# Four stages of a four-layer kernel reordered: gates first, keys and values turned early, attention waits by unit, and another order at the last attention's end

## The chip, the core and the metric

The kernel runs on one core of one Trainium2 chip. A core has five instruction streams that run side by side and meet only at semaphores: TensorE (matrix products, PE in the rows), VectorE (DVE), ScalarE (ACT), GpSimd (POOL) and SyncE (SP), which only issues transfers here. The metric is the device time of one execution in microseconds. Before the change three runs gave 2090.48, 2090.92 and 2097.49 us; the median is 2090.92 us.

## What is computed

Two blocks, one behind the other, of two layers each, on 256 tokens x and 256 context tokens, model width 1024, all in float32. Layers 0 and 1 (the first block) mix the tokens with a two-directional mLSTM, a gated spatial unit and a convolution; layer 2 mixes with windowed and dense attention, layer 3 with differential attention. Behind each mixer comes a SwiGLU feed-forward part. What the change touches, cut from the reference:

```python
def mlstm_inputs(p):
    q, k, v = heads(p[..., Q_OFF:K_OFF]), heads(p[..., K_OFF:V_OFF]) * HEAD_DIM ** -0.5, heads(p[..., V_OFF:O_OFF])
    g = p[..., GATE_OFF:SGU_OFF]                      # gates = (g0, log_sigmoid(g1), g2, log_sigmoid(g3))
def step(carry, inp):                                 # one chunk of 128 tokens of the mLSTM
    b = jnp.cumsum(fc, axis=-1)
    C_new = decay * C + einsum('bhsk,bhsv->bhkv', ks, vc)
    s = einsum('bhtk,bhsk->bhts', qc, kc) * exp(Dlog - m_t)
def one_block(args):                                  # layer 2
    p = _softmax(concatenate([s_c, s_w], axis=-1), sink_b)
    return einsum('bhgqk,bkhd->bqhgd', p[..., :n_ctx], v_ctx) + einsum('bhgqk,bkhd->bqhgd', p[..., n_ctx:], vw)
def _diff_attend(q, k, v, lam):                       # layer 3
    a = p[:, :, 0] - lam * p[:, :, 1]
    return einsum('bhqk,bkhe->bqhe', a, v)
def finish(o):
    return (_rms(o, subln_w) * (1.0 - lam_init)).reshape(o.shape[0], o.shape[1], -1) @ w_out
```

## The kernel before

The activations lie transposed in on-chip memory: 8 tiles of 128 rows (features) by 512 columns (256 tokens x, then 256 tokens of context). Layers 1 and 3 give out only the 256 tokens of x. Every large product is made of three products of rounded parts: weights and inputs are each split into a high part (ScalarE, `high_weights`) and a low part (VectorE, `low_weights`: the weight less its high part). The weights come in items of two tiles; ScalarE and VectorE split the item that comes next while TensorE multiplies the one before. In `coming_weights(L, e)` ScalarE's turn is at odd tiles e, VectorE's at even ones, and each half of an item has a semaphore count of its own.

There is no scheduler. Each engine's program is a Python function (`tensor_program`, `vector_program`, `scalar_program`, `pool_program`, `sync_program`), and its instructions run in the order in which they are written; an engine that waits holds back all that is behind it. The places that matter here:

- **mlstm_projection(L), layers 0 and 1.** 24 tiles e = 0 to 23. Behind tile 7 TensorE multiplies the gates' weights. ScalarE's `gate_activations` (five activations behind a table load) feed VectorE's `log_forget`, the scans `cumulated`, the running `maxima`, and then ScalarE's `row_exponents`, whose rows TensorE turns behind tile 15 (`gate_columns`). Tiles 12 to 19 (keys and values) are 512 wide in both layers. VectorE also applies the convolution's taps here (`conv_steps`). At the end stands a layer norm: means (`layer_norm_sums` part 0), centred (VectorE), squared (ScalarE), sums of squares (part 1), root, scaling, and silu (ScalarE).
- **mlstm(L).** First the keys and values of four heads are turned from features to tokens: TensorE turns into banks 0 to 3, VectorE copies the keys out, ScalarE the values; two heads fit into the banks at a time. Then the recurrent stage: TensorE spreads rows (64 x n), makes scores (128 x 128), outer and inner products, each in turn with VectorE's exponents and weighting, ScalarE's exponentials and GpSimd's scaled keys; modulation steps for later layers stand in between.
- **even_projection and even_mixer, layer 2.** Ten of the twelve projected tiles are normalised by head and rotated (three VectorE steps each, semaphore `rotated`). 24 units of attention follow, three to a tile (`kind` 0 to 2). For each: scores (TensorE), maximum (VectorE), exponential (ScalarE), reciprocal (VectorE), scaling of one half of the map by GpSimd and of the other by ScalarE (`even_weights`), turn, copy out, product. Units 0 to 2 are scored within the projection; the unit AHEAD = 3 further on is scored before unit n is turned.
- **odd_mixer, layer 3.** Behind the projection stand the last two maps (14 and 15), the products of heads 6 and 7, the squares, their bounding (`sub_bounded`) and their means (`sub_mean`) for heads 4 to 7, root and reciprocal (`sub_norm`), the spread of the factors over the rows (`sub_spread`), the normalised heads, their high (`odd_cut`) and low parts (`odd_low`), and the first half of the depth of the first four output tiles (`upper_mixed`).
- `keep_busy(b, n)` is n products of 128 x 128 into a bank that nobody reads.

In the names of the rows, `bank` is the accumulation memory, `big` and `scratch` are shared storage, `yT` and `rstd` hold squares, rows or statistics according to the stage, and `modulation_slots` holds attention's results in layer 3.

## Time and profile before

| | us |
|---|---|
| median of three runs | 2090.92 |
| lowest, highest | 2090.48, 2097.49 |
| profiled execution | 2094.34 |
| its span, from first to last instruction | 2092.9 |
| TensorE busy | 1999.8 (96%) |
| VectorE busy | 1394.4 (67%) |
| ScalarE busy | 1043.3 (50%) |
| GpSimd busy | 422.8 (20%) |
| mean granted TensorE clock | 0.993 |

Times in the rows are microseconds from the start of the span. A timeline row has start, duration, engine, line, operation, result <- inputs, shape, count, and in brackets the engine's idle time before it and the instruction that ended it. The lines of matrix products and turns are those of helpers (L780, L789), and so is L1526, a VectorE multiply-add. A float32 product of TensorE leaves two records, a turn one.

### The profile page before, as it was taken

What the parts mean: (1) busy time and instruction counts of PE and PEld (TensorE: products, weight loads), DVE (VectorE), ACT (ScalarE), POOL (GpSimd) and SP (SyncE); (2) the same over time, 40 slices, a digit from 0 to 9 for tenths busy, and PEclk for the clock granted to TensorE, in tenths of its full rate; (3) what the DMA queues carried; (4) which work ended last, traced back from release to release, by engine and by line L of the source; (5) the groups of instructions that cost most, each with busy time, mean ns of one, the idle gap of its engine ahead of it and who ended that gap; (6) DMA issues with size and microseconds to landing.
All of it is one profiled execution on the core that took longest, in us unless ns stands there. A gap on an engine that the chain in (4) does not pass through costs nothing.

```text
span 2092.9 us, 32728 instructions
## 1 busy us (share of the span) xinstructions
PE 1999.8 (96%) x12878; PEld 1683.1 (80%) x12878; DVE 1394.4 (67%) x2355; ACT 1043.3 (50%) x1948; POOL 422.8 (20%) x324
## 2 busy tenths in 40 slices
PE   6999999999999899999999999999999999999999
PEld 4776677888997777799986567798898877769999
DVE  4394647967987765655564674796798866666555
ACT  3445544542553555654455793454255256555443
POOL 1000415521541003200010241651254100000000
PEclk9999899999999999999999999999999999999999
DMA  9632521547458823556463102254832632114563
GB/s 337 227 141 81 172 70 50 193 136 258 147 172 258 302 84 108 196 185 197 144 199 121 61 2 89 81 187 117 273 101 89 227 110 73 61 61 157 166 208 115
DMA packets 276745, 311.65 MB, mean 149 GB/s; under 512 B 6128, under 2 KB 260208, under 8 KB 269424
## 3 DMA queue, kind: packets, MB, share of 16 engines
q1 hardware_dynamic: 271888, 304.90, 44.5%
q10 hardware_dynamic: 4704, 4.65, 0.7%
q8 instruction: 103, 1.69, 0.3%
q14 instruction: 50, 0.41, 0.1%
HBM read 308.48 MB, written 1.05 MB: 148 GB/s over the span
## 4 chain that ended last, share of the span: by engine, by line
PE 72%; DVE 13%; ACT 7%; POOL 3%; issue 3%; DMA 1%; ACTq 0%; DVEq 0%; POOLq 0%
PE bank L780 70%; DVE weights_low L1534 3%; PE bank L789 2%; ACT weights_high L2323 2%; DVE scratch L1526 1%; DVE weights_low L1915 1%; DVE yT L1526 1%; DVE input_low L1526 1%; DMA parameter_columns<-p_columns 1%; DVE big L2159 1%; ACT big L2856 1%; DVE big L1526 1%; DVE hidden_low L1929 1%; POOL token_sums_raw L673 0%; DVE token_sums L1920 0%
## 5 line engine op out<-in xcount | busy, mean ns | idle before, releaser
L780 PE MATMUL bank<-input_high,weights_high 128*128 128x256 f32 (+1 forms) x2336 | 749.4, 322 | 26.0 <-DVE scratch L1953 9.6
L780 PE MATMUL bank<-input_high,weights_low 128*128 128x256 f32 (+1 forms) x2336 | 736.0, 316 | 0.0
L780 PE MATMUL bank<-input_low,weights_high 128*128 128x256 f32 (+1 forms) x2336 | 714.5, 317 | 4.8 <-DVE input_low L1526 4.8
L1534 DVE TENSOR_TENSOR weights_low<-weight_slots,weights_high 128x1024 fp32r<-128x1024 f32 (+2 forms) x344 | 386.9, 1163 | 188.3 <-ACT weights_high L2323 188.0
L780 PEld LDWEIGHTS bank<-input_high,weights_high 128*128 128x128 f32 x2336 | 439.9, 188 | 83.4 <-issue 26.1
L780 PEld LDWEIGHTS bank<-input_low,weights_high 128*128 128x128 f32 x2336 | 434.0, 188 | 42.7 <-DVE input_low L1526 9.2
L780 PEld LDWEIGHTS bank<-input_high,weights_low 128*128 128x128 f32 x2336 | 440.0, 188 | 33.4
L2323 ACT ACTIVATE weights_high<-weight_slots 128x1024 fp32r<-128x1024 f32 (+2 forms) x348 | 314.5, 951 | 150.1 <-PE bank L780 137.0
L1915 DVE TENSOR_TENSOR weights_low<-weight_slots,weights_high 128x512 fp32r<-128x512 f32 x216 | 232.8, 1097 | 23.4 <-ACT weights_high L2601 21.5
L780 PE MATMUL bank<-hidden_high,weights_high 128*128 128x256 f32 (+1 forms) x704 | 238.5, 339 | 0.6 <-DVE weights_low L1534 0.4
L780 PE MATMUL bank<-hidden_high,weights_low 128*128 128x256 f32 (+1 forms) x704 | 237.4, 337 | 0.0
L780 PE MATMUL bank<-hidden_low,weights_high 128*128 128x256 f32 (+1 forms) x704 | 237.2, 337 | 0.0
L751 POOL TENSOR_TENSOR yT<-yT 128x256 f32<-128x256 f32 (+1 forms) x66 | 66.5, 1012 | 634.1 <-ACT yT L2349 504.4
L1526 DVE SCALAR_TENSOR_TENSOR xT<-bank,modulation,xT 128x256 f32<-128x256 f32 x144 | 64.4, 479 | 125.5 <-PE bank L780 124.7
L2601 ACT ACTIVATE weights_high<-weight_slots 128x512 fp32r<-128x512 f32 x216 | 129.3, 623 | 37.0 <-POOL weight_slots L696 19.0
L780 PEld LDWEIGHTS bank<-hidden_high,weights_high 128*128 128x128 f32 x704 | 132.1, 188 | 18.5 <-issue 1.9
L780 PEld LDWEIGHTS bank<-hidden_high,weights_low 128*128 128x128 f32 x704 | 132.1, 188 | 16.1
L780 PEld LDWEIGHTS bank<-hidden_low,weights_high 128*128 128x128 f32 x704 | 132.2, 188 | 15.8
L780 PE MATMUL bank<-token_sums,weights_high 128*128 128x256 f32 x576 | 105.2, 281 | 3.6 <-ACT scratch L2648 2.5
L691 POOL TENSOR_TENSOR weight_sum<-weight_slots 128x512 f32<-128x512 f32 x36 | 49.8, 1382 | 277.8 <-DVE weights_low L1915 135.6
L2349 ACT ACTIVATE yT<-xT 128x256 f32<-128x256 f32 (+1 forms) x64 | 32.9, 522 | 139.7 <-DVE xT L1526 134.2
L780 PEld LDWEIGHTS bank<-token_sums,weights_high 128*128 128x128 f32 x576 | 88.0, 188 | 5.0 <-ACT scratch L2648 3.4
(278 smaller groups left out, 2760.3 us busy)
## 6 DMA issues: line engine op xcount, KB each, us to landing
weight_slots<-w_gu SPq DMA_DIRECT2D x44, 1024.0 KB, 5.2
weight_slots<-ffn_w_in SPq DMA_DIRECT2D x44, 1024.0 KB, 5.2
modulation_slots<-p_modulation_rows SPq DMA_DIRECT2D x64, 512.0 KB, 4.7
modulation_slots<-mod_w SPq DMA_DIRECT2D x32, 1024.0 KB, 6.2
modulation_slots<-w_mod SPq DMA_DIRECT2D x28, 1024.0 KB, 6.3
weight_slots<-w_in SPq DMA_DIRECT2D x24, 1024.0 KB, 7.9
weight_slots<-w_down SPq DMA_DIRECT2D x16, 768.0 KB, 5.9
weight_slots<-ffn_w_out SPq DMA_DIRECT2D x16, 768.0 KB, 5.7
```

The source lines that it names most:

```text
L691: pool.tensor_tensor(m.weight_sum[:, :, :], a21, a22, ALU.add).then_inc(m.weights_added.sem, 1)
L751: pool.tensor_tensor(o, yT[:, 2 + q, t] if k == 1 else o, yT[:, 2 + i % 4, t], ALU.add).then_inc(m.square_joined.sem, 1)
L780: return pe.matmul(o, w, r, start=start, stop=stop, skip_group_check=shared)
L789: return pe.transpose(o, a, ident[0:a.shape[0], 0:a.shape[0]])
L1526: return stt(out=o, in0=a, scalar=s, in1=b, op0=op0, op1=op1)
L1534: tt(m.w_low[:, g % 2, c], m.ring[:, g % SLOTS, c], m.w_high[:, g % 2, c].bitcast(F32), ALU.subtract).then_inc(m.low_made.sem, 1)
L1915: tt(low, m.raw(run, j), high.bitcast(F32), ALU.subtract).then_inc(m.low_made.sem, 1)
L1929: tt(m.a_low[:, local, :], m.prod[:, f % 2, :], m.a_high[:, local, :].bitcast(F32), ALU.subtract).then_inc(m.hid_low.sem, 1)
L2159: dve.tensor_reduce(m.od_max[:, x % 2, a:a + 1], bank[2 + a][:, :], AX.X, ALU.max).then_inc(m.odd_max.sem, 1)
L2323: F(m.w_high[:, g % 2, c], m.ring[:, g % SLOTS, c], ACT.Copy).then_inc(m.high_made.sem, 1)
L2349: F(yT[:, 2 + k % 4, t], xT[:, k, t], ACT.Square).then_inc(m.squared.sem, 1)
L2601: F(m.split(j)[0], m.raw(run, j), ACT.Copy).then_inc(m.high_made.sem, 1)
```

## The change

1. Layer 1's gates: `gate_activations` stands ahead of tile 8's evacuation on ScalarE, and VectorE's low weights of the item that follows tile 10 stand ahead of the first scans.
2. Layers 0 and 1: the turns of heads 0 and 1 move between the last layer norm's two sums, with VectorE copying both their keys and values there; the values of heads 0 to 2 are copied by VectorE (semaphore `v_moved`), only those of head 3 by ScalarE. Behind the turns stand 14 `keep_busy` products.
3. Layer 2: the wait for all rotations is replaced by one per query tile; the first turn waits for the banks it needs. ScalarE's scaling of maps 0 and 1 moves ahead of unit 2's exponentials, with VectorE's second reciprocal ahead of it.
4. Layer 3: squares and bounds of heads 5 and 6 come earlier, cuts and low parts of heads 0 to 3 later, and the halves of the output tiles are spread between the means; the low weights of the second item stand inside the norm.

```diff
@@ TensorE, mlstm_projection and mlstm
-        for part in range(2):
-            layer_norm_sums(L, 1, part, n)
+        layer_norm_sums(L, 1, 0, n)
+        for h in range(2):
+            turn_keys_values(L, h)
+        layer_norm_sums(L, 1, 1, n)
+
+    def turn_keys_values(L, h):
+        for s, (tile, out_) in enumerate(((K_T, m.k_out), (V_T, m.v_moved))):
+            b = 2 * (h % 2) + s
+            if h > 1:
+                pe.wait_ge(*out_.at(L, h - 2))
+            else:
+                pe.wait_ge(*m.projected.at(L, 20 + b))
...
-        for h in range(HEADS):
...
+        for h in range(2, HEADS):
+            turn_keys_values(L, h)
+        keep_busy(5, 14)
         pe.wait_ge(*m.k_out.end(L))
+        pe.wait_ge(*m.v_moved.end(L))
         pe.wait_ge(*m.v_out.end(L))
@@ TensorE, layer 2
+        if n >= AHEAD and kind == 0:
+            pe.wait_ge(*m.rotated.at(2, 3 * (2 + n // 3) + 2))
...
+            elif half == 0:
+                pe.wait_ge(*m.head_root.end(2))
+            else:
+                pe.wait_ge(*m.rotated.at(2, 3 * (len(EVEN_NORMED) - 1)))
...
-        pe.wait_ge(*m.rotated.end(L))
@@ TensorE, layer 3
-        for h in (6, 7):
-            sub_mean(h)
-        upper_mixed(L, 0)
+        sub_mean(6)
+        upper_mixed(L, 0, (0,))
+        sub_mean(7)
+        upper_mixed(L, 0, (1,))
+        upper_mixed(L, 1, (0,))
         pe.wait_ge(*m.odd_keyed.end(0))
         for u in (2, 3):
             sub_spread(u)
-        upper_mixed(L, 1)
+        upper_mixed(L, 1, (1,))
@@ VectorE, layer 1 and both first layers
-            coming_weights(L, e)
+            if L == 0 or e != 10:
+                coming_weights(L, e)
...
+                    if s == 1 and L == 1:
+                        coming_weights(L, 10)
                     cumulated(L, (2 * s - 2, 2 * s - 1))
...
+        layer_norm(L, 1, 0, n)
+        for h in range(2):
+            keys_by_token(L, h)
+            values_by_token(L, h)
+        layer_norm(L, 1, 1, n)
@@ VectorE, layer 2 and layer 3
+            if e == 12:
+                even_reciprocal(1)
...
+        sub_bounded(5)
         odd_mix(14)
-        odd_low(0)
         odd_normalised(1)
         odd_reciprocals(15)
-        sub_bounded(5)
+        odd_joined(6)
         odd_mix(15)
-        odd_joined(6)
+        odd_low(0)
+        sub_bounded(6)
         odd_low(1)
-        low_weights(m.outp[L][1], range(1))
-        sub_bounded(6)
         odd_joined(7)
         sub_bounded(7)
-        sub_norm(1)
+        sub_norm(1, (0,))
+        low_weights(m.outp[L][1], range(1))
+        sub_norm(1, (1,))
@@ ScalarE
+                if s == 0 and L == 1:
+                    gate_activations(L)
                 projected_tile(L, e, ACT.Identity if s < O_T else ACT.Sigmoid, ...)
                 coming_weights(L, e)
-                if s == 0:
+                if s == 0 and L == 0:
                     gate_activations(L)
...
+            if e == 12:
+                for n in range(2):
+                    even_weights(n)
...
+        sub_square(5)
         odd_keys(13)
         odd_exponential(15)
+        odd_second(15)
+        odd_keys(14)
         odd_cut(0)
-        odd_second(15)
-        sub_square(5)
-        odd_keys(14)
+        sub_square(6)
+        odd_keys(15)
         odd_cut(1)
-        odd_keys(15)
         high_weights(m.outp[L][1], range(1))
-        sub_square(6)
         sub_square(7)
```

TensorE in layer 0, from the last norm's means to the first spread rows, before:

```order
654 L780 MATMUL bank<-scratch,mean_over 128x512 [waits sgu_tokens_out,convolution_steps]
655 L780 MATMUL bank<-scratch,mean_over 128x512
656 L780 MATMUL bank<-big,mean_over 128x512 [waits sgu_gated,layer_norm_activated]
657 L780 MATMUL bank<-big,mean_over 128x512 [waits layer_norm_activated]
658 L789 MATMUL bank<-ident,big 128x128 [waits projection_tiles_out]
659 L789 MATMUL bank<-ident,big 128x128 x15
660 L789 MATMUL bank<-ident,big 128x128 [waits keys_by_token]
```

and after:

```order
610 L781 MATMUL bank<-scratch,mean_over 128x512 x2
611 L790 MATMUL bank<-ident,big 128x128 x16
612 L781 MATMUL bank<-big,mean_over 128x512 x2
613 L790 MATMUL bank<-ident,big 128x128 x16
614 L781 MATMUL bank<-ident,mean_over_d 128x128 x14
615 L781 MATMUL bank<-yT,ident 128x512
```

Half of the 32 turns moved ahead of the sums of squares, and 14 fillers stand ahead of the spread rows.

ScalarE in layer 1, from the split of tiles 10 and 11's weights (tile 7 is evacuated just before it) to the split of the weights of tiles 12 and 13, before:

```order
500 L2323 ACTIVATE weights_high<-weight_slots 128x1024 [waits weight_tile_multiplied,weight_slot_filled3]
501 L2323 ACTIVATE weights_high<-weight_slots 128x1024
502 L2458 ACTIVATE big<-bank,parameter_columns,projection_scales 128x256 [waits weight_tile_multiplied]
503 L2313 ACT_TABLE_LOAD
504 L2406 ACTIVATE yT<-bank,parameter_columns 64x512 [waits gates_multiplied]
505 L2407 ACTIVATE yT<-bank,parameter_columns 64x512
506 L2409 ACTIVATE yT<-yT 64x512 [waits gate_activations]
507 L2411 ACTIVATE yT<-yT 64x512 [waits gate_activations]
508 L2413 ACTIVATE yT<-yT,ones_row 64x512 [waits gate_activations]
509 L2458 ACTIVATE big<-bank,parameter_columns,projection_scales 128x256 [waits weight_tile_multiplied]
510 L2323 ACTIVATE weights_high<-weight_slots 128x1024 [waits weight_tile_multiplied,weight_slot_filled0]
```

and after:

```order
500 L2359 ACTIVATE weights_high<-weight_slots 128x1024 [waits weight_tile_multiplied,weight_slot_filled3]
501 L2359 ACTIVATE weights_high<-weight_slots 128x1024
502 L2349 ACT_TABLE_LOAD
503 L2442 ACTIVATE yT<-bank,parameter_columns 64x512 [waits gates_multiplied]
504 L2443 ACTIVATE yT<-bank,parameter_columns 64x512
505 L2445 ACTIVATE yT<-yT 64x512 [waits gate_activations]
506 L2447 ACTIVATE yT<-yT 64x512 [waits gate_activations]
507 L2449 ACTIVATE yT<-yT,ones_row 64x512 [waits gate_activations]
508 L2494 ACTIVATE big<-bank,parameter_columns,projection_scales 128x256 [waits weight_tile_multiplied] x2
509 L2359 ACTIVATE weights_high<-weight_slots 128x1024 [waits weight_tile_multiplied,weight_slot_filled0]
```

Tile 8's evacuation moved behind the table load and the five gate activations.

VectorE at the end of layer 3's attention, from the maximum of map 15 to the last bounded square, before:

```order
1735 L2163 TENSOR_SCALAR big<-big 128x2 [waits odd_maxima,odd_exponentials]
1736 L1526 SCALAR_TENSOR_TENSOR big<-big 128x512 [waits odd_second_maps]
1737 L2224 TENSOR_TENSOR input_low<-modulation_slots,input_high 128x256 [waits mixed_high] x2
1738 L1526 SCALAR_TENSOR_TENSOR modulation_slots<-modulation_slots,lambda,bank 128x256 [waits sub_norm_spread]
1739 L1526 SCALAR_TENSOR_TENSOR modulation_slots<-modulation_slots,lambda,bank 128x256
1740 L2172 RECIPROCAL big<-big 128x2 [waits odd_maps_mixed,odd_second_maps,odd_exponentials]
1741 L2174 TENSOR_TENSOR big<-big,lambda 128x1 [waits odd_reciprocals]
1742 L2188 TENSOR_SCALAR xT<-xT 128x256 [waits sub_norm_squares]
1743 L1526 SCALAR_TENSOR_TENSOR big<-big 128x512 [waits odd_second_maps]
1744 L2183 COPY modulation_slots<-bank 128x256 [waits odd_products]
1745 L2224 TENSOR_TENSOR input_low<-modulation_slots,input_high 128x256 [waits mixed_high] x2
1746 L1534 TENSOR_TENSOR weights_low<-weight_slots,weights_high 128x1024 [waits weight_halves_high]
```

and after:

```order
1745 L2198 TENSOR_SCALAR big<-big 128x2 [waits odd_maxima,odd_exponentials]
1746 L2223 TENSOR_SCALAR xT<-xT 128x256 [waits sub_norm_squares]
1747 L1543 SCALAR_TENSOR_TENSOR big<-big 128x512 [waits odd_second_maps]
1748 L1543 SCALAR_TENSOR_TENSOR modulation_slots<-modulation_slots,lambda,bank 128x256 [waits sub_norm_spread]
1749 L1543 SCALAR_TENSOR_TENSOR modulation_slots<-modulation_slots,lambda,bank 128x256
1750 L2207 RECIPROCAL big<-big 128x2 [waits odd_maps_mixed,odd_second_maps,odd_exponentials]
1751 L2209 TENSOR_TENSOR big<-big,lambda 128x1 [waits odd_reciprocals]
1752 L2218 COPY modulation_slots<-bank 128x256 [waits odd_products]
1753 L1543 SCALAR_TENSOR_TENSOR big<-big 128x512 [waits odd_second_maps]
1754 L2259 TENSOR_TENSOR input_low<-modulation_slots,input_high 128x256 [waits mixed_high] x2
1755 L2223 TENSOR_SCALAR xT<-xT 128x256 [waits sub_norm_squares]
```

The bounded square of head 5 moved ahead of map 14's mix, the first low parts from ahead of map 15's mix to behind it, and the low weights away, into the norm.

## Rows read from the trace of the kernel before

**Rows 1.** The page: TensorE's busy time, its share of the span, instructions.

```profile
PE 1999.8 (96%) x12878; PEld 1683.1 (80%) x12878; DVE 1394.4 (67%) x2355; ACT 1043.3 (50%) x1948; POOL 422.8 (20%) x324
```

**Rows 2.** Stretches: length, busy time by engine, granted TensorE clock, DMA share, GB/s.

```profile
209.00:222.00 13.00, 12.26 (x35) 7.60 (x34) 6.16 (x18) 4.18 (x6) 3.50 (x6) 0.50 0.00 1
...
745.20:751.00 5.80, 5.74 (x14) 4.57 (x15) 5.50 (x13) 0.00 (x0) 0.00 (x0) 0.50 0.58 184
...
1178.00:1181.00 3.00, 3.00 (x12) 1.80 (x11) 2.31 (x6) 1.88 (x5) 1.02 (x2) 0.50 0.00 0
...
1868.00:1870.60 2.60, 2.60 (x7) 2.03 (x7) 1.43 (x2) 0.68 (x2) 0.00 (x0) 0.50 0.02 6
363.00:369.00 6.00, 3.04 (x25) 1.70 (x17) 5.05 (x9) 4.05 (x8) 0.94 (x1) 1.00 0.76 272
1352.00:1358.00 6.00, 3.51 (x26) 2.33 (x15) 5.05 (x9) 4.01 (x8) 0.90 (x1) 0.78 0.76 276
```

**Rows 3.** Timelines around layer 1's gates: TensorE, ScalarE, VectorE.

```profile
729.23 0.40 PE L780 MATMUL bank<-input_high,gate_weights_low 128*128 128x512 f32 x1
...
745.26 0.77 PE L780 MATMUL bank<-input_high,weights_high 128*128 128x512 f32 x1 [4.43 <-DVE weights_low L1534]
...
732.47 0.56 ACT L2458 ACTIVATE big<-bank,parameter_columns,projection_scales 128x256 f32<-128x256 f32 x1 [5.89 <-PE bank L780]
...
737.11 0.73 ACT L2413 ACTIVATE yT<-yT,ones_row 64x512 f32<-64x512 f32 x1
...
759.43 0.78 ACT L2458 ACTIVATE big<-bank,parameter_columns,projection_scales 128x512 f32<-128x512 f32 x1 [4.82 <-PE bank L780]
...
740.28 1.74 DVE L1671 TENSOR_TENSOR_SCAN big<-ones_row,yT 32x128 f32<-32x128 f32 x4
...
743.90 2.35 DVE L1534 TENSOR_TENSOR weights_low<-weight_slots,weights_high 128x1024 fp32r<-128x1024 f32 x2
...
754.38 2.35 DVE L1534 TENSOR_TENSOR weights_low<-weight_slots,weights_high 128x1024 fp32r<-128x1024 f32 x2
```

**Rows 4.** TensorE's timeline in layer 0, norm, turns and first recurrent steps.

```profile
201.48 1.98 PE L780 MATMUL bank<-big,mean_over 128*128 128x512 f32 x4 [1.44 <-ACT big L2437]
203.30 1.91 PE L789 MATMUL bank<-ident,big 128*128 128x128 f32 x16
206.96 0.66 PE L789 MATMUL bank<-ident,big 128*128 128x128 f32 x4 [1.75 <-DVE big L1805]
...
211.22 2.04 PE L780 MATMUL bank<-yT,ident 64*128 64x512 f32 x2 [0.74 <-issue]
...
223.20 1.16 PE L780 MATMUL bank<-big 128*128 128x128 f32 x8
```

**Rows 5.** VectorE's copies and ScalarE's silu there.

```profile
206.22 1.28 DVE L1805 COPY big<-bank 128x512 f32<-128x512 f32 x2
...
206.17 1.34 ACT L2449 ACTIVATE yT<-scratch,parameter_columns 128x512 f32<-128x512 f32 x2
```

**Rows 6.** TensorE's timeline: four filler products at another place.

```profile
695.00 1.16 PE L780 MATMUL bank<-ident,mean_over_d 128*128 128x128 f32 x8
```

**Rows 7.** Timelines in layer 1: first spread rows, and ScalarE's silu.

```profile
819.49 0.67 PE L780 MATMUL bank<-yT,ident 64*128 64x256 f32 x2 [0.73 <-DVE big L1805]
...
815.79 0.91 ACT L2449 ACTIVATE yT<-scratch,parameter_columns 128x256 f32<-128x256 f32 x2
```

**Rows 8.** Timelines in layer 2: scores of unit 3, exponentials of unit 4.

```profile
1176.47 0.66 PE L780 MATMUL bank<-big 64*128 64x512 f32 x1 [3.31 <-DVE big L2048]
...
1183.55 0.69 ACT L2766 ACTIVATE big<-bank,big 128x512 f32<-128x512 f32 x1 [0.52 <-DVE big L1526]
```

**Rows 9.** Timelines in layer 3: a mean, the last product, a normalised pair.

```profile
1865.48 0.62 PE L780 MATMUL bank<-xT,mean_over_d 128*32 128x256 f32 x2 [2.58 <-DVE xT L2188]
...
1867.53 3.56 PE L780 MATMUL bank<-modulation_slots,yT 128*128 128x256 f32 x8 [0.73 <-issue]
...
1878.07 0.87 DVE L1526 SCALAR_TENSOR_TENSOR modulation_slots<-modulation_slots,lambda,bank 128x256 f32<-128x256 f32 x2
```

47 lines of the change are left out of this document (24 added, 23 removed).

## The prediction

> **What bounds the kernel now.** The page comes first: TensorE is busy for 96% of the span, 1999.8 of 2092.9 us [rows 1]. So a change can pay in two ways only: fewer microseconds in which TensorE stands still, or fewer in which it runs at the lower of its two clock levels (1.2 instead of 2.4 GHz, shown as 0.50). Second come the busy times by stretch with the granted clock; there I looked for slices in which either happens. The change works at five places, and four of them have a stretch at 0.50: 209 to 222 us in layer 0, 745 to 751 in layer 1, 1178 to 1181 in layer 2, 1868 to 1870.6 in layer 3 [rows 2]. In each TensorE is busy almost throughout, so it is the slow clock that costs there, and the idle time stands just before it. Third, the timelines of the engines at these places say what ends each wait. Everywhere else TensorE's rows follow each other without a gap that the change touches, so what is won at a place reaches the end of the span undiminished, unless a later place uses it up.
>
> **Layer 1's gate chain.** TensorE has finished the gates' product at 729.6 us [rows 3]. ScalarE, though, has tile 8's evacuation ahead of the gate activations in its program and waits 5.89 us for that tile, so the last of the five activations ends at 737.84. VectorE's log-forget waits for it, and behind it the low halves of the weights of tiles 12 and 13 start only at 743.90; TensorE waits 4.43 us for them, until 745.26, and its clock then stands at 0.50 for 5.8 us [rows 2, 3]. After the change the activations start at 729.6. They take 3.5 us (the table load falls into the wait), so they end at 733.1. Tile 8's evacuation moves from 732.5 to 733.1; the first to want its bank is tile 12 at 740.8. ScalarE splits the weights after tile 9, about 735.8 to 737.7, and VectorE, which now has them ahead of the scans, makes the low halves by 739.1, 1.7 us before TensorE wants the first. The wait is gone, 4.4 us, and with it most likely the fall of the clock, 5.8 us at half rate, 2.9 us. What is late next is the following pair of tiles. Between the two pairs' low halves VectorE has 8.2 us of scans, taps and maxima (743.90 to 754.38, less 2.3 for the pair), and the two scans with their taps, 3.6 us (740.28 to 743.90), now stand there too [rows 3]. So the next pair starts at 739.1 + 11.8 = 750.9, and its first half is made at 752.1. TensorE wants it two tiles behind 740.8; a tile of 24 products takes 5.6 us at full clock (tile 13's from 753.8 to its evacuation at 759.43, rows 3), so at 752.0. I charge 0.3 us for this and for the row exponentials, which are as close. Sum: -7.0 us. Bounds: 4.0 if the clock falls all the same, 7.5 with no new wait.
>
> **Layer 0's keys and values.** Before: TensorE stands 1.44 us ahead of the squares' sums, turns two heads, stands 1.75 us, turns the other two, and begins the recurrent stage with the spread rows at 211.22 [rows 4]. After: 16 of the 32 turns (1.91 us) stand in the first gap, which they fill and overrun by some 0.3 us, so the sums end at 203.7. VectorE copies two heads' keys and values in 4 x 0.64 us [rows 5] between 201.3 and 203.9; it was idle there, and its next step, the norm at 204.9, waits for ScalarE. The 16 turns left follow without a wait, until 205.5. The stage may then begin when VectorE has copied three more tiles after the norm (206.4 + 3 x 0.65 = 208.4) and ScalarE the fourth value tile (silu until 207.4, now 0.3 later, + 0.6 = 208.3). But the 14 fillers stand ahead of it: four fillers, 8 records, last 1.16 us with the pipeline's end [rows 6], so one is about 0.27 us and 14 are 3.8 us. They end at 209.3, 0.9 us past what they cover. Start: 211.2 - 209.3 = 1.9 us. Then the clock. From 211.22 to the second scores at 223.20 are 12.0 us, of which 1.0 is the modulation step at full clock and 11.0 ran at 0.50 [rows 2, 4]. At full clock the work is 5.5 us; about 0.6 us comes back as waits for VectorE's exponents and weighting, whose durations don't shrink. That is 4.9 us. Sum: -6.9 us. Bounds: 2 if the clock falls in spite of the fillers, 8.5 if the fillers cost nothing. What then bounds this stage is TensorE again. GpSimd's key scaling starts earlier with the keys, and the modulation steps want their loads at the old spacing.
>
> The Trainium skill (TensorE: Matmul & The Clock Gate, "HAM oscillation — how this bites in real kernels") prices throttled time at one minus the clock ratio, here half. By that rule the 13.0 us at 0.50 in layer 0 would give back 6.5 us instead of 4.9, and the whole sum would be 22.2.
>
> **Layer 1's keys and values.** The same edit, with tiles half as wide. The stage begins at 819.49 [rows 7]; the clock held there. Sums of squares end at 813.7 (0.6 us of overrun, half of it under ScalarE's table load), turns at 815.4, fillers at 815.4 + 3.8 = 819.2. The copies would be ready at about 817.5 (silu over at 816.7 in [rows 7] and 0.2 later, one copy). So the fillers use up 1.7 of 2.0 us: -0.3 us. Bounds: 0.6 slower if overrun and fillers come out longer, 1.5 faster if they are shorter.
>
> **Layer 2's attention.** TensorE waits 3.31 us at 1176.47 for the end of the last rotated tile [rows 8], though unit 3 needs only a tile rotated long before. With a wait of its own, unit 3's scores start right after the last swap, at 1173.4. The new waits of the first turn (root done at 1170.8, first product of the last rotation at 1175.1) don't hold it: it comes at 1175.2. But from here on ScalarE is the one to watch. Its exponentials of unit 4 start at 1183.55 [rows 8]. Taking the two scalings of maps 0 and 1 (1.3 us) out of the way puts unit 3's at the time that VectorE's maximum allows: the rotation ends at 1176.3 as before, maximum and shift take 1.45, so 1177.8. Unit 4 follows after unit 3's 1.8 us, a scaling of 0.9 and a copy of 0.6, at 1181.1. That is 2.5 us ahead, and as ScalarE then stays busy nearly without a gap, 2.5 us is what reaches the end. Bounds: 1 and 3.6 (what TensorE alone would gain).
>
> **Layer 3's tail.** TensorE waits 2.58 us for a bounded square whose ScalarE and VectorE steps stand behind the cutting of finished heads, then 0.73 us ahead of the last product, which runs at 0.50 in 3.56 us [rows 2, 9]. After: square 5 falls into a ScalarE gap, map 15 is mixed at 1863.9, not 1866.1, its turn ends at 1864.6 and its copy at 1865.4. The product starts 2.1 us earlier and takes 1.8 at full clock: over at 1867.2, not 1871.0, 3.8 us ahead. Behind it the norm's chain sets the end. Half of an output tile (1.4 us) stands now between the last two means, and the low weights (1.22 us) between bound and reciprocal, where ScalarE's root takes 0.4; TensorE's second output tile waits 1 us for these low weights, with the spreads queued behind it. In return the tiles stand where TensorE idled. Working the chain through, the first normalised pair moves from 1878.07 [rows 9] to 1875.1, the last low half to 1878.6, and the first output tile's end from 1882.9 to 1879.0. Sum: -3.9 us; bounds 1.5 (clock falls again) and 4.5.
>
> Value copies on VectorE instead of ScalarE cost nothing: 0.64 against 0.60 us each, in VectorE's idle time. GpSimd's and SyncE's programs don't change at all.
>
> **The sum.** 7.0 + 6.9 + 0.3 + 2.5 + 3.9 = 20.6 us. The profiled execution took 2094.34 us, of which 1.4 lie outside the span, and the median of the runs is 2090.92, 3.4 under it; so 2070.3 by the median.
>
> **The rivals.** (a) *The clock falls elsewhere.* Layers 0 and 2 have the same stretch with the same idle time (3.0 and 2.5 of 6 us): at 363 us the clock held, at 1352 it fell [rows 2]. So a fall depends on more than the gap. If it falls in one of the two places with the most at stake, or in two new ones of 3 us, 5 to 9 us are lost: 2078. (b) *The gain moves behind another engine.* In layers 2 and 3 ScalarE and VectorE are the pace; if they win 1 and 1.5 us instead of 6.4 and layer 1's new wait is 1 us, it is 15 us: 2076. (c) *More than that:* the fall at 1352 goes too and the fillers cover fully: 24 us, 2067. (d) *It doesn't do what it says:* in the three large places the wait named is replaced by one as long on the same chain; only the fillers' clock is left: some 8 us, 2083. (e) *Slower:* the low level, once there, stays through layer 0's recurrent stage. Rows speak for it: from 209 to 222 TensorE was busy for 12.26 of 13.0 us and the clock stayed at 0.50 all the same [rows 2]. If the fillers don't prevent the fall, they cost 7.6 instead of 3.8 us, layer 0's gain is lost, and 33 us of the stage behind 223 would take up to 30 more: +14 us, 2105. It decides from some 14 us of further low clock gained against (0.5 us each) only if all of layer 0 is lost; slower overall needs 27 us or more. Against it: in layer 1 the same stage held 1.00 with more idle time. The Trainium skill (same page, "What's actually happening") says that activity releases the throttle; these 13 us speak against that at least for this mix of matmuls.
>
> **How the numbers follow.** Forecast 0.56, own range 2066 to 2075; (a) 0.16; (b) 0.13; (c) 0.07; (d) 0.06; (e) 0.02. The likeliest is 2070. With the bounds of the terms and (a) to (c) inside, the range is 2065 to 2080. Faster by over 0.5%, about what can be told from no change here, is below 2080.5: 0.90. Within it 0.07, slower 0.03.
>
> **What would show it.** Right: no stretch at 0.50 at the four places; tile 12 of layer 1 without a wait; the 14 fillers in 3.8 us with the copies over before they end in both layers; ScalarE's unit 3 exponentials about 2 us closer to the last swap; layer 3's last product in 1.8 us. Wrong: a wait of over 1 us for low weights at tile 14, ScalarE idle in layer 2's attention, or a stretch at 0.50 in either recurrent stage.

## The result, and the profile after

Four runs of the changed kernel gave 2071.65, 2071.7, 2074.5 and 2077.42 us, a median of 2073.1 us against 2090.7 for four of the kernel before; the ratio is 0.9912, with a 95% interval of 0.989 to 0.9934. Measured a second time beside the experiments, it took 2073.35 us (four runs, 2072.18 to 2073.66) against 2093.03 us (19 runs), ratio 0.990 [0.9879, 0.9921]. So the change saves 18 to 20 us, 0.9 to 1.0%. The likeliest time was put at 2070 us and the range at 2065 to 2080: the time lies in the range, 3.1 us over the forecast.

The profiled execution of the changed kernel took 2071.7 us (span 2070.2), 22.7 us less in span than that of before. The profile's page of the kernel after, TensorE's busy time first (compare [rows 1]): 15.0 of the 22.7 us are less idle time, 7.7 less busy time, although the fillers alone add 6.4 us to the latter.

```profile
PE 1992.1 (96%) x12934; PEld 1681.0 (81%) x12934; DVE 1398.3 (68%) x2361; ACT 1039.7 (50%) x1942; POOL 424.1 (20%) x324
```

Stretches of the kernel after, columns as in [rows 2] (TensorE, its weight loads, VectorE, ScalarE, GpSimd). The first four are the four places of [rows 2], the last two the layer 0 and layer 2 token sums:

```profile
209.00:222.00 13.00, 12.91 (x76) 7.53 (x74) 9.38 (x31) 6.09 (x12) 7.36 (x10) 1.00 0.24 81
733.00:739.00 6.00, 6.00 (x31) 4.95 (x30) 5.74 (x16) 2.46 (x3) 0.00 (x0) 1.00 0.57 175
1158.00:1161.00 3.00, 1.96 (x13) 1.28 (x14) 2.82 (x9) 2.52 (x11) 0.00 (x0) 1.00 0.00 0
1846.00:1849.00 3.00, 3.00 (x14) 2.10 (x15) 1.27 (x4) 1.97 (x5) 0.00 (x0) 1.00 0.00 0
359.00:363.00 4.00, 3.93 (x20) 3.93 (x21) 3.56 (x7) 2.43 (x6) 2.56 (x2) 0.57 0.99 407
1335.00:1341.00 6.00, 4.66 (x37) 4.46 (x38) 6.00 (x7) 4.01 (x10) 3.68 (x3) 1.00 1.01 405
```

The low clock is gone at all four places. One stretch is new, at 359 us in layer 0, where the kernel before held 1.00, and the one in layer 2's token sums (1352 to 1358 before) is gone.

**Layer 0** (compare [rows 4]). TensorE's timeline after: the first two heads' turns, the sums of squares, 28 filler records, spread rows, second scores.

```profile
199.91 1.91 PE L790 MATMUL bank<-ident,big 128*128 128x128 f32 x16
201.65 1.88 PE L781 MATMUL bank<-big,mean_over 128*128 128x512 f32 x4
...
205.12 3.29 PE L781 MATMUL bank<-ident,mean_over_d 128*128 128x128 f32 x28
208.34 1.12 PE L781 MATMUL bank<-yT,ident 64*128 64x512 f32 x2
...
215.50 0.71 PE L781 MATMUL bank<-big 128*128 128x128 f32 x4
```

There is no wait from the means to the spread rows. The fillers stand from 205.12 to 208.34, 3.22 us; the last value copy of VectorE is over at 208.17.

**Layer 1** (compare [rows 3, 7]). ScalarE, VectorE and TensorE after: the gate activations' last, tile 8's evacuation, low weights of the items 12/13 and 14/15, and TensorE at tile 14.

```profile
725.32 0.73 ACT L2449 ACTIVATE yT<-yT,ones_row 64x512 f32<-64x512 f32 x1
726.07 0.56 ACT L2494 ACTIVATE big<-bank,parameter_columns,projection_scales 128x256 f32<-128x256 f32 x1
...
729.71 2.36 DVE L1551 TENSOR_TENSOR weights_low<-weight_slots,weights_high 128x1024 fp32r<-128x1024 f32 x2 [1.13 <-ACT weights_high L2359]
...
743.81 2.35 DVE L1551 TENSOR_TENSOR weights_low<-weight_slots,weights_high 128x1024 fp32r<-128x1024 f32 x2
...
745.17 0.47 PE L781 MATMUL bank<-input_high,weights_high 128*128 128x512 f32 x1 [0.25 <-DVE weights_low L1551]
```

The wait of 4.43 us has become one of 0.25 us, one item later.

**Layer 2 and layer 3** (compare [rows 8, 9]). Scores of unit 3 (1156.84) follow the last swap without a wait; those of unit 4 (1160.46) wait 0.92 us for ScalarE. ScalarE's exponentials of unit 3 start at 1161.14, those of unit 4 at 1164.11. Layer 3's last product takes 1.9 us, and TensorE waits 0.90 us for the low weights that now stand inside the norm.

```profile
1156.84 0.69 PE L781 MATMUL bank<-big 64*128 64x512 f32 x1
...
1160.46 0.69 PE L781 MATMUL bank<-big 64*128 64x512 f32 x1 [0.92 <-ACT big L2804]
...
1161.14 0.70 ACT L2804 ACTIVATE big<-bank,big 128x512 f32<-128x512 f32 x1
...
1164.11 0.71 ACT L2804 ACTIVATE big<-bank,big 128x512 f32<-128x512 f32 x1
...
1846.01 1.97 PE L781 MATMUL bank<-modulation_slots,yT 128*128 128x256 f32 x8 [0.73 <-issue]
...
1853.18 0.36 PE L781 MATMUL bank<-input_high,weights_high 128*128 128x256 f32 x1 [0.90 <-DVE weights_low L1551]
...
1856.29 0.87 DVE L1543 SCALAR_TENSOR_TENSOR modulation_slots<-modulation_slots,lambda,bank 128x256 f32<-128x256 f32 x2
```

**Where the 22.7 us are.** TensorE executes nearly the same rows in both kernels. So each row of before can be paired with its row of after, and its start less that of the other is a running account: it is flat where nothing changes and steps where something does. A time after plus the account ahead of a place is called the time on the scale of before.

| from (before, us) | account | step | forecast |
|---|---|---|---|
| layer 0, second scores 223.20 / 215.50 | 7.7 | +7.7 (2.9 start, 4.8 clock) | 6.9 |
| layer 1 begins, 698.95 / 691.81 | 7.1 | -0.6 | 0 |
| behind the gates, row exponents turned, 770.66 / 756.46 | 14.2 | +7.1 | 7.0 |
| layer 1 recurrent stage, 819.49 / 804.16 | 15.3 | +1.1 | 0.3 |
| end of layer 1's feed-forward part, 1097.86 / 1081.35 | 16.5 | +1.2 | 0 |
| layer 2 attention, 1181.49 / 1161.52 | 20.0 | +3.5 | 2.5 |
| layer 3 begins, 1676.00 / 1656.67 | 19.3 | -0.6 | 0 |
| behind layer 3's tail, 1900.05 / 1877.41 | 22.6 | +3.3 | 3.9 |

### The profile page after: what moved, and what is told of

It is laid out like the page before. It is cut to its first block, busy times and chain, and to the rows that moved or that the text cites. A ratio compares the mean times of both kernels' runs of the same rounds, so it can differ in the third digit from the quotient of the medians.

```text
span 2070.2 us, 32856 instructions
## 1 busy us (share of the span) xinstructions
PE 1992.1 (96%) x12934; PEld 1681.0 (81%) x12934; DVE 1398.3 (68%) x2361; ACT 1039.7 (50%) x1942; POOL 424.1 (20%) x324
## 4 chain that ended last, share of the span: by engine, by line
PE 70%; DVE 16%; ACT 6%; POOL 3%; issue 3%; DMA 2%; ACTq 0%; DVEq 0%; POOLq 0%
PE bank L781 68%; DVE weights_low L1551 3%; PE bank L790 2%; ACT weights_high L2359 2%; DVE weights_low L1948 2%; DVE scratch L1543 1%; DVE yT L1543 1%; DVE input_low L1543 1%; DMA modulation_slots<-p_modulation_rows 1%; DMA parameter_columns<-p_columns 1%; DVE modulation_slots L1577 1%; DVE big L2194 1%; DVE big L1543 1%; ACT big L2895 1%; DVE xT L1543 1%
```

## The experiments

Twelve runs were made, one of them of the changed kernel again. The four parts were taken one by one on the kernel before, as were the two halves of part 1 and the fillers; and from the changed kernel part 1, part 2 or the fillers were taken out. Each was measured beside the kernel before, whose medians in the three groups of runs were 2093.86, 2093.03 and 2094.0 us. The ratios with their intervals are not the quotients of the medians (gates alone: 0.9963 against 0.9976), and how they are formed is not recorded; in microseconds the two differ by up to 3. "Clock loss" below is the time multiplied by one less its mean granted clock: 15.4 us on average over the 20 runs of before beside the first four kernels, 4.1 over the four runs of the changed kernel in its second measurement. The steps of the account are taken between the rows of the table above where nothing else is said.

### Each part alone

Gates alone: ScalarE's and VectorE's halves of part 1.

> The kernel before with part 1 alone: layer 1's gate activations ahead of tile 8's evacuation, and the low weights of tiles 12 and 13 ahead of the scans. My theory (the ledger of the two traces puts 7.1 us on this place): TensorE waits 0 us ahead of tile 12, about 0.25 us ahead of tile 14, no stretch at clock 0.50 around 745 us, and the row exponentials' turns of layer 1 start 7.0 us earlier against the gates' product; the whole is 7 us shorter, with nothing given back behind. Rival (the parts need each other: the gates are only free because layer 0 left its clock and buffers in another state): the clock falls somewhere behind in layer 1 and 3 us or less arrive at the end.

Measured 2088.78 us against 2093.86 (ratio 0.9963 [0.9946, 0.998]), 5.1 us. In its trace the account steps by 7.0 us at the gates: no wait at tile 12, 0.25 us at tile 14. But 1.1 us had gone ahead of the place, at the end of layer 0's feed-forward part, some 1.0 us go with a stretch at the low clock from 815 to 820 us that the kernel before did not have, and 1.3 us at layer 2's attention, where the low clock lasts longer than before (table below); 3.7 us are left at the end of the span. The theory on the place held; "nothing given back behind" didn't. A fall behind the place in layer 1 was the rival's; its bound of 3 us at the end was not.

Keys and values alone:

> The kernel before with part 2 alone: keys and values turned early and 14 fillers, layers 0 and 1. My theory: layer 0's second scores start 7.7 us earlier (2.9 of start, 4.8 of clock), the end of layer 0 keeps 7.1 of it, layer 1's stage gains another 1.1; in all 8 to 9 us. The fillers take 3.2 us in each layer. Rival one (the prediction's sizes): 3.8 us for the fillers, 7.2 in all. Rival two (the clock falls elsewhere once it holds here): a fall of 3 to 6 us at layer 0's token sums, near 363 us, that reaches the end; 3 to 5 us in all.

Measured 2089.21 against 2093.86 us (0.9971 [0.9958, 0.9984]), 4.7 us. The account reads 8.0 us behind layer 0's stage, where it is 7.7 in the changed kernel, and steps by 1.1 in layer 1 as there. But 1.3 us go at 675 us, where TensorE waits for low weights whose splitting stands on VectorE behind a step that waits for a load; and the low clock lasts 7 to 8 us at 1167 and 1860, where in the kernel before it was 4 to 5 (counted in whole slices of 1 us); these two cost 1.4 and 0.6 us. The trace of keys and values alone, VectorE's wait for the load and TensorE's behind it, then three stretches with columns as in [rows 2]:

```profile
673.41 1.23 DVE L1570 SCALAR_TENSOR_TENSOR modulation_slots<-modulation_slots 128x1024 f32<-128x1024 f32 x1 [1.66 <-DMA modulation_slots<-p_modulation_rows]
...
674.56 1.56 DVE L1544 TENSOR_TENSOR weights_low<-weight_slots,weights_high 128x640 fp32r<-128x640 f32 x2
...
675.52 0.47 PE L781 MATMUL bank<-hidden_high,weights_high 128*128 128x512 f32 x1 [1.17 <-DVE weights_low L1544]
```

```profile
737.00:745.00 8.00, 5.73 (x15) 4.54 (x16) 7.70 (x18) 0.33 (x1) 0.00 (x0) 0.57 0.43 132
1167.00:1175.00 8.00, 7.01 (x23) 3.71 (x24) 3.21 (x9) 5.68 (x19) 2.80 (x3) 0.57 0.00 0
1860.00:1868.00 8.00, 6.92 (x20) 3.63 (x19) 3.57 (x9) 3.94 (x7) 0.00 (x0) 0.57 0.00 0
```

So the sizes at the place were those of the theory. The total by the medians was that of rival two, though the interval of the ratio, 3 to 9 us, holds the theory's 8 as well; and the fall at layer 0's token sums which that rival named (358 to 363 here) was not what cost it: see below.

Layer 2 alone:

> The kernel before with part 3 alone: a wait per query tile, ScalarE's scaling of maps 0 and 1 earlier. My theory after the result: 3.5 us, of which 3.4 from the start of unit 3's scores and 0.8 from the clock, less 0.5 of a new wait for ScalarE behind unit 3's scores. Rival (the prediction): ScalarE sets the pace and only 2.5 us arrive behind unit 4's exponentials.

Measured 2089.99 us (0.9972 [0.9961, 0.9983]), 3.9 us, and 3.5 at the place in the trace: unit 3's scores start 3.4 us earlier, 0.5 us are lost to a wait for ScalarE's scaling of the map and come back from the clock. The theory held in the trace. The interval of the times, 3.6 to 8.2 us, lies clear of the rival's 2.5 and just above the theory's 3.5.

Layer 3 alone:

> The kernel before with part 4 alone: another order at layer 3's end. My theory after the result: map 15's turn starts 2.2 us earlier, the last product ends 3.8 us earlier, of which 0.8 are given back to the low weights inside the norm; 3.3 us at the end. Rival (the prediction): 3.9 us. Rival two (the clock falls at the last product in spite of the shorter waits): 1.5 us.

Measured 2091.65 us (0.9989 [0.9978, 1.0001]), 2.2 us. The account steps by 3.3 us at the tail (3.7 ahead, 7.0 behind). The runs can't tell 3.3 from 3.9 us; the trace gives the former, with a wait of 0.92 us for the low weights. Its trace shows something else: with layer 0's program untouched, the long stretch at the low clock in layer 0 did not appear, but one from 811 to 822 us in layer 1 did.

### The changed kernel again, and without one part

> The changed kernel itself, unedited, beside the others: four runs of it spread from 2071.7 to 2077.4 us with mean granted clocks of 0.996 to 0.999. The four parts alone gave 5.1, 4.7, 3.9 and 2.2 us by their medians, 15.9 in all. If the parts merely add, the changed kernel is 16 us under the kernel before, some 2078 us; if they help each other (a stretch at the low clock that one part removes no longer appears at another part's place), it is 18 to 23 us under it, 2071 to 2076 us, with a mean clock of 0.998 or more.

Measured 2073.35 us, 19.7 under the kernel before, clock loss 4.1 us. By the medians the four parts alone come to 15.9 us (5.1, 4.7, 3.9 and 2.2). Leaving parts out of the changed kernel:

> The changed kernel without part 2. Alone, part 2 gave 4.7 us by medians, although its own places gained 8.8 in its trace: 1.3 went to waits at the end of layer 0's feed-forward part, 0.9 each to longer stretches at the low clock at the two attention places. My theory (the parts help each other, since parts 3 and 4 remove the waits that those longer stretches start from): taken out of the changed kernel it costs more than it gives alone, 7 to 9 us, so 2080.5 to 2082.5 us. Rival (the parts simply add): 4.7 us, 2078 us.

Measured 2083.56 us (0.9952 [0.9936, 0.9967]): 10.2 us over the changed kernel's second measurement (9.2 if each is set against the kernel before beside it), where the part alone gave 4.7. Its clock loss is 12.0 us on average. In the trace the stage of layer 0 runs at 0.51 again (209 to 223 us) and the account against the changed kernel reads 8.0 behind it.

> The changed kernel without part 1. Alone, part 1 gave 5.1 us by medians. My theory (mutual help, through the clock): out of the changed kernel it costs 7 to 8 us, 2080.5 to 2081.5 us, with a wait of 4.4 us at tile 12 and a stretch at 0.50 behind it. Rival (the parts simply add): 5.1 us, 2078.5 us.

Measured 2082.13 us (0.9943 [0.9924, 0.9961]): 8.8 us over the changed kernel (7.8 each against its own kernel before), where part 1 alone gave 5.1; the wait of 4.43 us is back, with the low clock from 739 to 746 us. Its profiled execution is the slowest of its four; there layer 3's last product takes 3.02 us instead of 1.97, although part 4 is in.

By the medians all three comparisons point to parts that help each other, by some 3 to 6 us. By the ratios the first points the other way: the four parts come to 22.0 us (7.7, 6.1, 5.9 and 2.3), the changed kernel to 20.9; the other two give surpluses of 4.8 and 1.3 us. Each has an interval of 2 to 4 us to either side. So that the parts help each other is not shown.

### Which half of part 1 does it

ScalarE's half alone:

```diff
@@ ScalarE, mlstm_projection, kernel before
+                if s == 0 and L == 1:
+                    gate_activations(L)
                 projected_tile(L, e, ...)
                 coming_weights(L, e)
-                if s == 0:
+                if s == 0 and L == 0:
                     gate_activations(L)
```

> The kernel before with only ScalarE's half of part 1: the gate activations of layer 1 ahead of tile 8's evacuation; VectorE's low weights stay behind the first scans. My theory (ScalarE's order alone is the cause): log-forget runs 4.7 us earlier, the low weights of tiles 12 and 13 start 4.7 us earlier than 743.9, and their first half is there at 740.4, 0.3 us before TensorE wants it; so the wait of 4.43 us is gone without VectorE's part, and the pair behind comes at 749.7 + 1.2, so there is no new wait of 0.25 us at tile 14 either: 7.3 us at this place. Rival (both orders are needed): a wait of 1 us or more at tile 12 remains, and the clock falls with it: 3 us.

Measured 2089.21 against 2093.03 us (0.998 [0.9965, 0.9995]), 3.8 us. In the trace there is no wait at tile 12 nor at tile 14, no low clock there, and the account steps from 3.0 to 10.4: 7.4 us. VectorE's timeline, low weights of both items, the first half of the first there some 0.2 us before TensorE wants it at 737.58:

```profile
730.09 0.68 DVE L1526 SCALAR_TENSOR_TENSOR yT<-yT 64x512 f32<-64x512 f32 x1 [4.69 <-ACT yT L2413]
...
736.12 2.35 DVE L1534 TENSOR_TENSOR weights_low<-weight_slots,weights_high 128x1024 fp32r<-128x1024 f32 x2
...
746.60 2.35 DVE L1534 TENSOR_TENSOR weights_low<-weight_slots,weights_high 128x1024 fp32r<-128x1024 f32 x2
```

VectorE's half alone (`coming_weights(L, 10)` ahead of `cumulated`, nothing else):

> The kernel before with only VectorE's half of part 1: the low weights of tiles 12 and 13 ahead of the first scans of layer 1, ScalarE's order as before. My theory (ScalarE's order is the cause, VectorE's move is dispensable): log-forget still waits for ScalarE until 737.9, the low weights start at 740.3 and their first half is there at 741.5, so 0.7 us of the 4.43 us stay at tile 12; the scans that were overtaken push the next pair to 754.4 as before, its first half to 755.6, and TensorE, which would want it at 752.7, waits some 3 us at tile 14. The two waits come to 3.5 to 4 us: the place gains 0 to 1 us and the clock still falls near it. Rival (the wait at tile 12 was the whole cost): a gain of 4 to 7 us.

Measured 2088.7 against 2094.0 us (0.9979 [0.9967, 0.9991]), 5.3 us. TensorE's waits are near those expected, 0.81 and 2.68 us:

```profile
738.68 0.47 PE L780 MATMUL bank<-input_high,weights_high 128*128 128x512 f32 x1 [0.81 <-DVE weights_low L1534]
...
752.79 0.47 PE L780 MATMUL bank<-input_high,weights_high 128*128 128x512 f32 x1 [2.68 <-DVE weights_low L1534]
```

But the expectation was wrong on the clock: it held at 1.00 behind both, so the place gains 3.7 us (0.9 of wait, the rest of clock), not 0 to 1. In this trace one wait of 4.4 us was followed by no fall once it was cut in two. By their times the two halves can't be told apart (3.8 and 5.3 us, intervals some 2.5 to 3 us to either side); the traces do it: ScalarE's order alone removes both waits and gives 7.4 us, VectorE's leaves 3.5 us of wait. So the expected cause stands, ScalarE's order; VectorE's move is dispensable, and with it comes the new wait at tile 14.

### The fillers

```diff
@@ TensorE, mlstm, changed kernel
-        keep_busy(5, 14)
```

> The changed kernel without the 14 fillers in layers 0 and 1. My theory (the fillers hold the clock): layer 0's spread rows start 0.2 us earlier, but the clock is at 0.50 for 3 to 14 us there, and the second scores come 1.5 to 5 us later than 215.5; layer 1's stage starts 1.1 us earlier; in all 1 to 4 us slower than the changed kernel. Rival (the earlier turns alone hold the clock, since they close the gaps ahead of the sums): clock 1.00 there, and 1.3 us faster than the changed kernel, all of it in layer 1.

Measured 2076.75 us, 3.4 over the changed kernel; clock loss 8.8 instead of 4.1 us. Its timeline and clock, without fillers:

```profile
208.34 1.25 PE L781 MATMUL bank<-yT,ident 64*128 64x512 f32 x2 [2.99 <-DVE scratch L1830]
209.52 2.07 PE L781 MATMUL bank<-big 128*128 128x128 f32 x8
211.52 3.78 PE L781 MATMUL bank<-yT,ident 64*128 64x512 f32 x4
```

```profile
209.00:222.00 13.00, 13.00 (x46) 7.49 (x44) 5.47 (x17) 4.87 (x8) 3.91 (x5) 0.61 0.09 11
```

The spread rows start at 208.34, to the hundredth where they start with the fillers, so these cost nothing in layer 0. They are worth 4.4 us of clock there and cost 1.0 us in layer 1, which was 1.0 us faster without them and kept its clock. The theory came out as expected, and the rival is refuted in this trace. It is one trace, of a stretch that comes and goes (see the clock over all traces below); but in all five traces with the earlier turns and the fillers (the changed kernel twice, keys and values alone, all but gates, the variant) the clock held from 205 to 222 us.

The fillers added to the kernel before, with nothing moved:

> The kernel before with only the 14 fillers added, behind the last turns, with nothing moved. In the trace of before the low clock begins at 208 us, 2.5 us ahead of the place of the fillers. My theory (the gaps ahead of them set off the fall, and the fillers come too late): the low clock is there as before, the fillers take 3.2 us at full and up to 6.4 at half clock less 0.7 of cover, and layer 0's second scores come 2.5 to 5.7 us later than before, layer 1's 2.5 us later: 5 to 8 us slower than before. Rival (busy time behind the gaps is what counts): the clock returns to 1.00 by 214 us, and the two losses of 2.5 us are set against 3 to 5 us of clock: 0 to 2 us slower.

Measured 2096.35 us (10 runs) against 2093.03, ratio 1.0007 [0.9992, 1.0021]: 3.3 us more by the medians, a difference that the interval of the ratio doesn't bear out. The spread rows start 3.0 us later and layer 1's stage 2.3 us later. The low clock lasted from 208 to 212 us only, so the result lies between theory and rival. The run doesn't settle whether the fillers ended the stretch, since layer 3 alone had one of the same length there without them.

### A variant

```diff
@@ changed kernel, VectorE's half of part 1 undone, and:
-        keep_busy(5, 14)
+        keep_busy(5, 14 if L == 0 else 9)
```

> The changed kernel with two edits: VectorE's half of part 1 undone, and 9 fillers instead of 14 in layer 1 (14 stay in layer 0). My theory: no wait for low weights at tiles 12 to 15 of layer 1 (0.25 us won), and layer 1's recurrent stage starts 1.1 us earlier against the sums ahead of it, since the copies are over at 803.0 while the fillers end at 804.2 now; 1.3 us in all, 2072.0 us by the median. Rival (14 fillers are needed in layer 1 to hold the clock): a stretch at 0.50 in layer 1's recurrent stage and no gain, or up to 4 us slower.

Measured 2074.83 us (five runs, 2069.57 to 2076.42; ratio to before 0.9899 [0.9883, 0.9916]): no difference from the changed kernel that the runs can tell. In the trace the two edits are worth 0.2 and 0.9 us and the clock held in layer 1's stage with 9 fillers. But the same trace had the low clock at 250 to 255 and 837 to 842 us and a wait of 1.07 us for low weights at 677 us, which cost 1.3, 1.2 and 1.3 us, none of it at a place of the edits.

### The clock over all traces

Stretches whose granted clock is under 0.97 in slices of 1 us, from TensorE's busy times by stretch, with the microseconds of the span at which they stand. The clock loss here is that of the profiled execution, not the mean of the runs:

| kernel | stretches at the low clock | clock loss |
|---|---|---|
| before | 208-223, 744-752, 1177-1182, 1355-1359, 1867-1871 | 15.4 |
| gates alone | 208-222, 815-820, 1170-1178, 1351-1355, 1863-1867 | 15.4 |
| keys and values alone | 358-363, 737-745, 1167-1175, 1348-1352, 1860-1868 | 13.7 |
| layer 2 alone | 208-223, 744-752, 1352-1356, 1864-1868 | 13.6 |
| layer 3 alone | 207-211, 739-744, 811-822, 1173-1177 | 10.2 |
| fillers alone | 208-212, 256-260, 365-369, 744-752, 853-857, 1177-1185, 1870-1878 | 17.1 |
| ScalarE's half | 257-261, 363-367, 840-845, 1165-1172, 1346-1350, 1858-1865 | 13.6 |
| VectorE's half | 253-261, 1168-1176, 1349-1353, 1861-1865 | 10.2 |
| all but keys and values | 209-223, 1346-1350 | 8.6 |
| all but gates | 250-258, 739-746, 844-849, 1858-1862 | 10.2 |
| no fillers | 209-220, 1339-1343 | 6.9 |
| changed kernel, both times | 359-363 | 1.7 |
| variant | 250-255, 837-842, 1339-1343 | 5.1 |

At three of the four places the low clock goes with the wait. The wait of 4.43 us ahead of tile 12 stands in six traces (before; keys and values, layer 2, layer 3 and fillers alone; all but gates), and all six have a stretch at the low clock there; the eight others have none. The wait of 3.31 us at layer 2's attention stands in the seven traces without part 3, and all seven have the stretch; the seven with part 3 have none. Layer 3's last product took 3.56 to 3.75 us in the seven traces without part 4 and 1.96 or 1.97 us in six of the seven with part 4, 3.02 us in the other (all but gates).

Layer 0 is different. Its program is the same in seven of the traces (before; gates, layer 2 and layer 3 alone; both halves; all but keys and values). Four have the long stretch there, one a short one, two none there but one at 253 to 261 us. The same 13 us with ScalarE's half alone, where the clock held; compare the first line of [rows 2], 12.26 us busy and 0.50:

```profile
209.00:222.00 13.00, 12.18 (x73) 7.82 (x71) 8.31 (x25) 7.70 (x13) 6.60 (x9) 1.00 0.25 81
```

## Why the prediction held, point by point

**Layer 1's gates, 7.0 forecast, 7.1 measured.** Each step held: activations behind the gates' product, no wait at tile 12, a new one at tile 14 of 0.25 where 0.3 was charged, the clock kept. What the prediction did not see is that VectorE's half was not needed: it took the four scans and taps as overtaken work that had to be charged, and didn't ask what ScalarE's half gives by itself. That gave 7.4 us in its trace.

**Layer 0's keys and values, 6.9 forecast, 7.7 measured.** The clock term was 4.9 and is 4.8. Start was 1.9 and is 2.9. Of the difference 0.6 us are the fillers: they were priced at 0.27 us each from a row of four with the pipeline's end in it [rows 6]; 28 records took 3.22 us, 0.23 a filler. The other 0.4 us are the turns, over at 205.12 where 205.5 was forecast. So the fillers end at 208.34, right behind the last copy, and not 0.9 us past it. By the rule of the Trainium skill that the prediction gave beside its own figure (TensorE: Matmul & The Clock Gate, "HAM oscillation — how this bites in real kernels": throttled time by one less the clock ratio) the 13.0 us would have given back 6.5. Only 11.0 of them lie behind the first spread rows; for these the rule gives 5.5 us, and 4.8 came back, so here it is 0.7 us too high. VectorE's steps between the products do not shrink: four exponents took 1.12 us in both traces.

**Layer 1's keys and values, 0.3 forecast, 1.1 measured.** The same step, the same price: 14 fillers are 0.6 us shorter than charged, and the turns ahead of them end 0.2 us sooner.

**Layer 2, 2.5 forecast, 3.5 measured.** Unit 3's exponentials start at 1161.14; with the account of 16.25 ahead of the place that is 1177.4 on the scale of before, where 1177.8 was forecast. Unit 4's start at 1180.4 on the same scale, not 1181.1: 0.4 us for the earlier start, 0.3 because the steps between are shorter than the durations that I added up. The step that failed is the bound: what reaches the end is not what ScalarE wins at unit 4 (3.2 us), for TensorE, with its clock kept, won 3.5, and ScalarE's later exponentials move with TensorE's rows.

**Layer 3, 3.9 forecast, 3.3 measured.** The last product ended 3.8 us earlier, as forecast, and TensorE waited 0.90 us for the low weights, 1 us forecast. Mis-sized was the chain behind: the first normalised pair starts at 1856.29, with the account of 19.3 ahead of the place at 1875.6 on the scale of before, not 1875.1.

**Between the places.** Two losses of 0.6 us at the ends of layers 0 and 2 (a wait for ScalarE of 0.87 us became 1.48 and 1.20 us) were not foreseen, nor a gain of 1.2 us that the change did not make (last section). The three cancel, which is luck: the terms at their places come to 22.7 us where 20.6 were forecast, and the spans of the pair differ by 22.7.

**Rival (a), the clock falls elsewhere,** came true in a harmless form: one stretch moved from layer 2's token sums to those of layer 0. It costs nothing at either place. The account dips from 7.7 to 6.6 us in the stretch and is back at 7.7 behind it, because the waits for VectorE that stand around it (0.47 and 0.88 us before) shrink by as much. Timeline of the kernel before, behind its stretch at full clock:

```profile
368.90 0.51 PE L780 MATMUL bank<-token_sums,weights_high 128*128 128x256 f32 x2 [0.47 <-DVE scratch L1945]
...
375.70 0.39 PE L780 MATMUL bank<-input_high,weights_high 128*128 128x256 f32 x1 [0.88 <-DVE scratch L1953]
```

**Rival (c), more than that,** named two conditions. The fall at 1352 is gone, and the fillers cover fully in layer 0 but end 1.1 us past the last copy in layer 1. The 22.7 us of the pair lie between the forecast's 20.6 and its 24.

**Where the 3.1 us between 2070.0 and 2073.1 come from.** The sum of the terms was 20.6 us; the second measurement gives 19.7 and the profiled pair 22.7. The step that was off is the last one, "3.4 under it; so 2070.3 by the median". The profiled execution was taken for one above the typical time and the median of three for the typical one. It was the other way round: 54 further runs of the kernel before have medians of 2093.0 to 2094.0 us, which the profiled 2094.34 us fits, and only 9 of the 54 are at 2091 us or under. 2094.34 less 20.6 would have been 2073.7. The difference is within the noise all the same: the interval of the first measurement, 14 to 23 us, holds 20.6. That the pair of traces gives more than the runs has a reason in the clock. The profiled execution of the changed kernel lost 1.7 us to it, its runs 4.1 on average; the profiled one of the kernel before lost 15.4, as its runs did. That is 2.4 of the 3.0 us between 22.7 and 19.7.

**Right or wrong for the right reason?** The mechanism held at all five places, and the sum holds. The clock's part of it was read from one trace as if it were fixed. For layer 1's gates, layer 2's attention and layer 3's last product the other traces bear this out: the low clock came each time the wait was there, and once at the last product without it. For layer 0 they don't: in seven traces of the same program the stretch, worth 4.8 us, was there in full four times, so that the traced one had it to give back was in part luck. What the changed kernel does reliably is to leave few stretches at all: its runs have clocks of 0.996 to 0.999, those of the kernel before 0.988 to 0.996. Stretches also appear or grow at other places (815, 811, 250, 837, 1167, 1860 us), but each kernel has been traced in a single execution; what decides where one comes stays open, and so does whether the parts together give more than one by one.

## What to carry to other kernels

Pair the rows of one engine in two traces and follow the difference of their starts: it separates what an edit does at its place from what is given back behind it, to a few tenths of a microsecond, where the runs scatter by several. Before an instruction order is changed on two engines, price each half alone: here ScalarE's, one call moved by one line, carried all of the largest forecast term in its trace. Before a stretch at the low clock is subtracted, look for it in several traces of the same program: at three places here it came every time, at the fourth four times in seven, and such a one needs a chance besides a price. And subtract a sum that was read from a trace from that execution's time.

## What the runs showed of the hardware

The same program with the same idle time ahead (waits of 1.44, 1.75 and 0.42 us in both) ran at a granted clock of 0.50 in one execution and at 1.00 in another: layer 0, 209 to 222 us, TensorE busy for 12.26 us in the kernel before and 12.18 with ScalarE's half alone. The spread of the kernel before is mostly such differences in clock: its fastest run (2089.74 us) has a mean clock of 0.995, its slowest (2101.8 us) 0.988.

A second effect is smaller and does not show in the granted clock. In layer 1's feed-forward part the steady products of 128x256 followed each other every 117.8 ns before and every 116.7 ns after, both with TensorE busy throughout and a clock of 1.00, over some 160 us; that is the step of 1.2 us in the account. A hundred microseconds of it, before and then after: 851 and 860 records in the same time (some records are missing from either).

```profile
900.00:1000.00 100.00, 100.00 (x851) 100.00 (x850) 56.47 (x73) 46.77 (x71) 4.45 (x6) 1.00 0.61 190
```

```profile
900.00:1000.00 100.00, 100.00 (x860) 100.00 (x859) 55.93 (x71) 46.82 (x72) 4.43 (x6) 1.00 0.62 190
```

Neither pitch belongs to a kernel: with the gates alone the slow one was in layer 1, with layer 3 alone and with ScalarE's half in layer 3 (where the rows had not changed), in all but gates in both, in the other nine traces in neither. No run here shows a cause for it. It is worth 1.2 to 1.8 us a time, which is more than some edits here.
